# Forgetting attention: the order of turns, scores, values and masks on TensorE

## The reference

```
q, k, v, g, f_logit = split(x @ w_in)
qh, kh = rms_norm(heads(q)), rms_norm(heads(k))
c = cumsum(log_sigmoid(f_logit + b_f))
s = qh kh^T / sqrt(64) + (c_t - c_s)          # per head
p = softmax(where(causal, s, -1e30))
o = (p @ v) * sigmoid(g);   h = o @ w_out
```

## Time and profile before

| | |
|---|---|
| median of 3 runs | 1349.88 us |
| profiled execution | 1350.16 us, span 1348.1 us |
| TensorE matmul / weight load busy | 1334.4 us (99%) / 1092.7 us (81%) |
| VectorE / ScalarE / POOL busy | 454.5 / 480.0 / 529.8 us |
| mean DMA rate | 89 GB/s |
| granted clock of TensorE | 0.999 of full speed over the span |

### The profile page before, as it was taken

The page is one execution under the profiler, slowest core; times in us unless marked ns, Lnnn a source line. Parts: engine busy times, 40 slices in busy tenths (PEclk is TensorE's granted clock), DMA queues, the critical chain, the costliest instruction groups (busy, mean ns, idle before and its releaser), DMA issues.

```text
span 1348.1 us, 17988 instructions
## 1 busy us (share of the span) xinstructions
PE 1334.4 (99%) x6943; PEld 1092.7 (81%) x6943; DVE 454.5 (34%) x857; ACT 480.0 (36%) x759; POOL 529.8 (39%) x421
## 2 busy tenths in 40 slices
PE   9999999999999999999999999999999999999997
PEld 7888877788888888888787877677898888888886
DVE  4364446771111111011643554545621111110105
ACT  3413266533222223211365554644332222222120
POOL 4422433334444444543352332323244444435440
PEclk9999999999999999999999999999999999999999
DMA  6301121314333332323123212313133333333221
GB/s 213 123 32 63 63 94 63 95 38 119 95 94 94 95 101 90 137 94 109 47 84 94 63 33 63 95 63 95 32 110 110 94 94 94 94 109 107 107 84 63
DMA packets 141540, 119.55 MB, mean 89 GB/s; under 512 B 5808, under 2 KB 120720, under 8 KB 141456
## 3 DMA queue, kind: packets, MB, share of 16 engines
q1 hardware_dynamic: 141216, 118.10, 27.9%
q10 hardware_dynamic: 240, 0.31, 0.1%
HBM read 116.20 MB, written 2.10 MB: 88 GB/s over the span
## 4 chain that ended last, share of the span: by engine, by line
PE 96%; DVE 2%; issue 1%; ACT 0%; DMA 0%; POOL 0%; SPq 0%; DVEq 0%; ACTq 0%; POOLq 0%
PE banks L561 28%; PE banks L563 28%; PE banks L562 28%; PE banks L989 2%; PE banks L1132 2%; PE banks L1167 2%; PE banks L1148 1%; PE banks L674 1%; PE banks L1080 1%; PE banks L1007 1%; PE banks L1067 1%; PE banks L1140 1%; PE banks L1118 0%; DMA x_res<-in_x_dram 0%; PE banks L1094 0%
## 5 line engine op out<-in xcount | busy, mean ns | idle before, releaser
L1281 POOL TENSOR_TENSOR w_lo<-w_raw,w_hi 128x512 fp32r<-128x512 f32 x417 | 529.6, 1299 | 786.9 <-ACT w_hi L1328 523.7
L561 PE MATMUL banks<-xT_lo,w_hi 128*128 128x512 f32 (+2 forms) x1024 | 383.7, 375 | 0.9 <-DVEq L1688 0.7
L563 PE MATMUL banks<-xT_hi,w_hi 128*128 128x512 f32 (+2 forms) x1024 | 380.0, 371 | 0.0
L562 PE MATMUL banks<-xT_hi,w_lo 128*128 128x512 f32 (+2 forms) x1024 | 379.9, 371 | 0.0
L1328 ACT ACTIVATE w_hi<-w_raw 128x2048 fp32r<-128x2048 f32 (+1 forms) x106 | 198.2, 1869 | 174.5 <-PE banks L563 145.6
L561 PEld LDWEIGHTS banks<-xT_lo,w_hi 128*128 128x128 f32 (+1 forms) x1024 | 191.4, 187 | 35.7 <-issue 3.3
L563 PEld LDWEIGHTS banks<-xT_hi,w_hi 128*128 128x128 f32 (+1 forms) x1024 | 191.3, 187 | 34.0
L562 PEld LDWEIGHTS banks<-xT_hi,w_lo 128*128 128x128 f32 (+1 forms) x1024 | 191.5, 187 | 32.6
L1960 DVE TENSOR_TENSOR banks<-silu_g,banks 128x512 f32<-128x512 f32 x44 | 30.6, 696 | 402.3 <-PE banks L563 402.3
L561 PE MATMUL banks<-w_lo,xT_hi 128*128 128x512 f32 (+1 forms) x352 | 135.9, 386 | 1.6 <-ACT q_raw L1350 0.7
L561 PE MATMUL banks<-w_lo,hT_hi 128*128 128x512 f32 x352 | 137.1, 390 | 0.0
(11 more groups left out here) (196 smaller groups left out, 1214.6 us busy)
## 6 DMA issues: line engine op xcount, KB each, us to landing
w_raw<-in_ffn_w_dram SPq DMA_DIRECT2D x92, 512.0 KB, 4.4
w_raw<-in_ffn_w_dram SPq DMA_DIRECT2D x20, 1024.0 KB, 4.9
w_raw<-in_even_w_in_dram SPq DMA_DIRECT2D x13, 1024.0 KB, 4.8
w_raw<-in_fox_w_in_dram SPq DMA_DIRECT2D x16, 512.0 KB, 4.4
w_raw<-in_fox_w_in_dram SPq DMA_DIRECT2D x8, 1024.0 KB, 5.6
w_raw<-in_even_w_out_dram SPq DMA_DIRECT2D x4, 1024.0 KB, 4.9
w_raw<-in_fox_w_out_dram SPq DMA_DIRECT2D x4, 1024.0 KB, 4.9
x_res<-in_x_dram SPq DMA_DIRECT2D x4, 512.0 KB, 7.1
```

Source lines behind the costliest of these rows:

```text
L561: mm(acc, l_hi, r_lo, start=first, stop=False)
L562: mm(acc, l_lo, r_hi, start=False, stop=False)
L563: return mm(acc, l_hi, r_hi, start=False, stop=final)
L1281: ins = nc.gpsimd.tensor_tensor(w_lo[c % RING][:, a:a + n], w_raw[c % RAW][:, a:a + n], w_hi[c % RING][:, a:a + n].bitcast(F32), ALU.subtract)
```

## The change

Only TensorE's program is touched. The masks leave `pair_scores` for a function of their own; a step issues the turns of s-2 first, then scores and bias of s, then the values, then the masks of s. Values are issued for two units, s-4 and s-3, in every even step from 4 to 30; from step 31 on one unit, s-3, in each step. Odd steps below 31 issue none. The lists of ScalarE, VectorE, POOL and SP stay as they are.

```diff
-                for m, acc in enumerate(accs):
-                    close_bank(("fs", s, m), mm(acc[:, n - P:n], ident_bf[:, :], fox_mask[:, :],
+
+            def pair_masks(s):
+
+                n = (s % NT + 1) * P
+                for m, b in enumerate(SCORE_BANKS[s % 3]):
+                    close_bank(("fs", s, m), mm(psum[b][:, n - P:n], ident_bf[:, :], fox_mask[:, :],
                                                 start=False, stop=True))
...
+            def values_of(s):
+
+                if s >= F_UNITS - 1:
+                    return [s - 3]
+                return [s - 4, s - 3] if s >= 4 and s % 2 == 0 else []
...
+                if 2 <= s < F_UNITS + 2:
+                    turn_pair(s - 2)
                 if s < F_UNITS:
                     pair_scores(s)
-                if 2 <= s < F_UNITS + 2:
-                    turn_pair(s - 2)
-                if s >= 3:
-                    pair_values(s - 3)
+                for u in values_of(s):
+                    pair_values(u)
+                if s < F_UNITS:
+                    pair_masks(s)
```

## The result

| | before | after |
|---|---|---|
| median | 1349.77 us (4 runs, 1349.45 to 1350.01) | 1373.01 us (4 runs, 1372.01 to 1373.09) |
| span of the profiled execution | 1348.1 us | 1371.0 us |
| granted clock over the span | 0.999 | 0.996 |

The ratio is 1.0171, 95% interval 1.0158 to 1.0183: 23 us slower. Forecast were 16 us slower, with a range of 6 to 24.

The account below looks back on a forecast made before the run. TensorE, busy 99% of the span, was taken to bound the kernel. Switches saved 6.1 us, waits added 22.4, net +16.3 on a median of 1349.88, so 1366 us was forecast, range 1356 to 1374.

Parts of the forecast that it names:

- (c): Turned heads one GEMM piece behind an even or late step wait for the turned-probability copy: 3.0 us added.
- (e): Behind step 10 the second GEMM piece waits for a bank that ScalarE's late head copy frees: 1.2 us added.
- (f): Turns of units 29 and 30 wait for copies of 28 and 29 behind one piece of cover: 1.3 us added.
- switches saved: Fewer changes of TensorE's array tile, mostly in fourteen pairs of steps at 0.43 us each: 6.1 us removed.
- (a): At six steps turns directly behind turned heads wait for ScalarE's two copies to free bank 3: 7.3 us added.
- (b): Turns wait for ScalarE's copy of the previous unit's turned probabilities, at five steps and slightly at three: 5.7 us added.
- (d): Steps 19 to 21: VectorE's in-order wait for values delays a ScalarE chain and the turns: 3.9 us added.
- Rivals 1 and 2: First: waits hidden, only switches count, 1344, chance 0.06; second: waits of some 6 us balance within 0.2%, chance 0.04.
- Rival 3: Only bank 3's waits count, 13.0 us, without the later chains: +7, 1357 us; chance 0.25.
- Rival 4: VectorE's stall spreads from step 17 on and units 25 to 31 wait too: another 10 us, 1376; chance 0.10.

Follow-up runs that it names:

- Experiment 6: Kernel before, with values of two units in every second step and VectorE waiting for values only where it reads them; old order otherwise: 1345.81 us, 0.9971.
- experiment 9: Changed kernel, but at the six steps with turned heads the scores come first and the turns stand behind the masks: 1361.81 us, 1.0089 of before.
- experiment 1: Changed kernel, but VectorE waits for a unit's values only where it reads them; TensorE's order stays: 1367.39 us, 1.0130 of before.
- experiment 2: Kernel before, with only the turns moved ahead of the scores; masks behind the bias, values of one unit a step: 1363.40 us, 1.0101.
- experiment 8: Kernel before, with values of two units in every second step, old order otherwise, VectorE still waiting for values in every step: 1354.54 us, 1.0035.
- (7): Kernel before, with each step's one-unit values between bias and masks, turns last, old order from step 31, VectorE waiting as before: 1349.39 us, 0.9996.
- experiment 3: Changed kernel with the turns last: scores, bias, values of two units in even steps, masks, turns: 1353.40 us, 1.0027 of before.
- 10: Kernel before, with values paired, VectorE waiting only where it reads, and values between bias and masks at seven steps, elsewhere behind turns: 1344.81 us, 0.9963.

## Why the prediction was right, and where it was too small

The direction, the mechanism and the places were right, and the range held; the sum was 7 us short. All waits below are read from starts that follow one another, less the steady distance; those that the kernel before had in the same place (0.3 in (c), 1.3 in (e), 0.6 in (f)) are taken off.

| term | forecast | measured |
|---|---|---|
| switches saved | -6.1 | -6.1 (what is left: the waits and the clock, 29.1, less 23.0) |
| (a) turned heads, then turns | 7.3 | 8.1: six times 1.33 to 1.39, step 22 too |
| (b) copy of the probabilities | 5.7 | 6.4: 1.00 to 1.23 five times, 0.24 to 0.44 three times |
| (c) turned heads behind a short cover | 3.0 | 4.7 |
| (d) VectorE's hold, unit 19 | 3.9 | 3.8, and 2.4 by the clock |
| (e) GEMM banks | 1.2 | 2.2 |
| (f) tail | 1.3 | 1.5 |
| sum | 16.3 | 23.0 in the stretch |

- The rows' prices of switches held. The -6.1 of the table is only a remainder, but the prices were found where they can be read: bias to values 0.15 as taken, and the entries of the values fell from 31 to 17. Experiment 6 shows an entry and an exit by themselves, 0.37 to 0.39 us for 0.35.
- (a) is shown by experiment 9: turns moved behind scores at six steps, 11.2 us. I had counted step 22 at 0.8, arguing that TensorE would be late there anyway. It was not late with respect to ScalarE's copies, which start when the turned heads end; the wait was whole. Step 22 and the time from copy to turns (next point) are the miss of this term.
- (b) has the steps of the forecast and was low by about 0.1 us at each. The trace says where that comes from: I had taken 0.06 us from the end of a copy to the first matmul that waits for it. For GEMM behind GEMM that is so (0.05: L1362 ends at 789.79, L561 starts at 789.84), but turns and turned heads started 0.14 to 0.15 behind ScalarE's copy at every one of their waits. So did the one such wait of turned heads in the kernel before (850.27). At the 14 waits of (a) and (b) this is 1.2 us. What makes the difference is left open.
- (c) was short by 1.7 us: I took the differences of the kernel before. The turned heads behind steps 6 and 14 waited 0.53 instead of 0.3, behind step 18 1.36 for 0.9, behind step 19 1.30 for 1.1, those in 23 0.92 for 0.4, and one I had not listed (behind step 4) 0.33. VectorE's hold accounts for part of it: with VectorE free (experiment 1) the wait behind step 18 is 0.49 and those behind 6 and 14 are 0.40. Those behind 4 and 19 hardly change, and that in 23 grows to 1.28, so for these the cause is open.
- (d) The chain from the values of unit 16 was read rightly from the rows: 7.25 less 0.3 forecast, 6.94 measured. What I missed was its effect on the clock; the forecast had it only as a condition in the last line. It is the largest single miss, 2.4 us. A wait of its own for unit 20 (0.5) does not show: its turns, at step 22, wait 1.33 as at the other steps of (a).
- Rivals 1 and 2 fell by every run with turns ahead. Rival 3 fell: the chains of (c) to (e) did come. Rival 4 fell as well: from step 25 to 30 no unit waits, two pieces are cover enough.
- The Trainium skill's rule on rotating banks (Perfetto Trace Analysis, Optimizing Tensor Performance, Matmuls) is borne out: two groups of one bank, back to back, cost 1.3 us each; with the scores between them (the kernel before, and experiment 9) that wait is gone.
- The Trainium skill (TensorE: Matmul & The Clock Gate, section Why this matters for your kernels) warns of gaps in which the clock goes back to its lower level. The trace agrees that a gap can do it: the one of 4.05 us did, as the windows show. The page speaks of a single gap; the fall of experiment 1, behind waits none of which is over 1.33 us, it does not cover.

The parts of the change, by the runs: turns ahead alone +13.7 (experiment 2); pairs with VectorE held +4.7 (8), with VectorE free -4.0 (6); masks behind the values, and the turns behind both, -0.4, within noise (7). They do not add up: 13.7 + 4.7 - 0.4 is 18.0, and all together cost 23.2. Putting the turns last in the changed kernel gives back 19.6 (3), more than their 13.7 alone. The turns' place costs more when values and masks are late too.

## What to carry to other kernels

An order that saves switches of the array must keep what the old order used as cover: count, for each bank and buffer, the time between its reader's start and the next writer, and put other work between two groups of the same bank. An in-order engine that waits for something it does not use is free only while that thing is early; moving its producer back by a step makes it a stall of everything queued behind it. Here pairing two units, with a wait less on VectorE, gave 4.0 us, and 4.9 with late masks at seven steps; the part that brought no saving of its own, the turns' place, cost 13.7 us alone and 19.6 with the others.

## What the runs showed that I had not expected

- The clock's fall does not need one long gap. In the changed kernel it came in a gap of 4.05 us and cost 2.4 us; in experiment 1 it came behind two waits of about 1.3 us close together, and in experiment 3 behind one of 2.0. In each of the three TensorE had worked at 1.00 for hundreds of microseconds before. The profiled executions of experiments 2, 6, 8 and 10 keep 1.00 through the stretch, experiment 8 with a wait of 2.7 us, so the length of the longest wait alone doesn't say whether it falls; what does is left open. It may not fall in every execution of a kernel either: of the four of experiment 1 three have a clock of 0.997 over the span, the fourth 0.999 and 1.2 us less than the profiled one. In experiment 8 two of the executions that were not profiled have 0.997 and 0.9 to 1.1 us more than the profiled one at 0.998. Whether those held a fall was not profiled.
- VectorE's idle wait costs 8.7 us with the turns in their old place and 5.6 with them ahead (7.6 and 5.5 in the stretch of the profiled executions, the second with a fall of the clock on either side), so its cost can't be carried from one order to another.
